# Front buffers in halves of ring slots, low parts written in place, and another form of router and first gather

## What is computed

```python
x1 = x + merged @ w_out
h2 = rms_norm(x1, norm2_g, NORM_EPS).reshape(B * S, D)
logits = (x2 @ w_router + b_router).astype(jnp.float32)      # x2 is h2
top_vals, top_idx = lax.top_k(logits, TOP_K)                  # 4 of 32
top_w = jax.nn.softmax(top_vals, axis=-1)
for e in range(N_EXPERTS):
    a = clamped_swiglu(x2 @ w_up[e] + b_up[e])
    out = out + combine[:, e:e + 1] * (a @ w_down[e] + b_down[e])
return x1 + y
```

## Time and profile before

| | |
|---|---|
| median of 3 runs | 1201.33 us (1199.94 to 1201.79) |
| profiled execution, its own time | 1200.07 us |
| its span, first to last instruction | 1198.3 us |
| PE busy | 1132.7 us (95%) |
| DVE, ACT, POOL busy | 387.5, 279.0, 81.7 us |
| bytes read from HBM | 448.12 MB |
| mean rate, rate from 300 us on | 376, 426 to 427 GB/s |

### The profile page before, as it was taken

How to read it: one execution, slowest core, us unless ns; L and a number is a source line. 1 busy time by engine, 2 the same in 40 slices (tenths; PEclk the granted TensorE clock), 3 DMA queues, 4 the chain that set the end, 5 groups by cost and what they waited for, 6 DMA issues and landing times.

```text
span 1198.3 us, 13630 instructions
## 1 busy us (share of the span) xinstructions
PE 1132.7 (95%) x5603; PEld 534.7 (45%) x5603; DVE 387.5 (32%) x711; ACT 279.0 (23%) x432; POOL 81.7 (7%) x98
## 2 busy tenths in 40 slices
PE   8999999999999999999999998999999899999887
PEld 7789988884333333333333333333333333333332
DVE  5767765653222222222222222222222222222222
ACT  6765454442111111111112111111111111111110
POOL 6424350000000000000000000000000000000000
PEclk9999999999999999999999999999999999999999
DMA  8454569868999999999999999999999999999994
GB/s 318 144 176 143 164 222 349 323 246 368 426 426 427 428 427 427 427 426 426 427 427 428 427 427 427 427 427 426 427 428 427 428 426 427 427 426 426 427 427 190
DMA packets 51466, 449.99 MB, mean 376 GB/s; under 512 B 4610, under 2 KB 4738, under 8 KB 26836
## 3 DMA queue, kind: packets, MB, share of 16 engines
q1 hardware_dynamic: 49936, 447.76, 90.4%
q10 hardware_dynamic: 1476, 1.42, 0.5%
HBM read 448.12 MB, written 1.05 MB: 375 GB/s over the span
## 4 chain that ended last, share of the span: by engine, by line
PE 62%; DMA 21%; SPq 8%; DVE 4%; ACT 1%; issue 1%; another core or an unknown queue 1%; POOL 1%; DVEq 0%; POOLq 0%; ACTq 0%
PE aux L1569 23%; DMA ring<-w_up_dram 20%; PE aux L1637 12%; PE acc L1419 12%; SPq L450 8%; PE aux L1500 3%; PE acc L1412 3%; PE acc L1559 2%; PE aux L1512 1%; DVE w_lo L857 1%; PE aux L1589 1%; PE aux L1619 1%; DVE pick_w L1122 1%; POOL rstd L532 1%
## 5 line engine op out<-in xcount | busy, mean ns | idle before, releaser
L1569 PE MATMUL aux<-ring,xgT 128*64 128x512 f32 x2048 | 462.1, 598 | 46.7 <-DMA ring<-w_up_dram 46.0
L1569 PEld LDWEIGHTS aux<-ring,xgT 128*64 128x64 f32 x2048 | 142.8, 137 | 339.7 <-issue 244.3
L1637 PE MATMUL aux<-ring,aT 128*64 128x512 f32 x1024 | 232.2, 596 | 0.0
L1185 DVE TENSOR_SCALAR glu<-aux 128x512 f32<-128x512 f32 x32 | 22.1, 691 | 396.5 <-PE aux L1569 396.5
L857 DVE TENSOR_TENSOR w_lo<-raw,w_hi 128x1024 fp32r<-128x1024 f32 x80 | 104.3, 1324 | 49.5 <-ACT w_hi L648 49.5
L1637 PEld LDWEIGHTS aux<-ring,aT 128*64 128x64 f32 x1024 | 68.5, 136 | 115.6 <-issue 110.1
L824 ACT ACTIVATE sig<-glu 128x512 f32<-128x512 f32 x32 | 20.2, 630 | 411.8 <-DVE glu L1185 411.8
L648 ACT ACTIVATE w_hi<-raw 128x1024 fp32r<-128x1024 f32 x80 | 84.1, 1059 | 88.3 <-PE acc L1419 72.9
L830 ACT ACTIVATE y_hi<-aux,slot_w 128x512 fp32r<-128x512 f32 x32 | 22.0, 687 | 259.6 <-PE aux L1637 259.6
L1419 PE MATMUL acc<-w_hi,hT_hi 128*128 128x512 f32 x188 | 75.7, 403 | 1.4 <-DVE hT_lo L869 1.3
L1419 PE MATMUL acc<-w_hi,hT_lo 128*128 128x512 f32 x188 | 73.4, 390 | 0.0
(11 more groups left out here) (281 smaller groups left out, 1023.7 us busy)
## 6 DMA issues: line engine op xcount, KB each, us to landing
ring<-w_up_dram SPq DMA_DIRECT2D x128, 2048.0 KB, 48.7
ring<-w_down_dram SPq DMA_DIRECT2D x64, 2048.0 KB, 49.0
raw<-w_in_dram SPq DMA_DIRECT2D x25, 1024.0 KB, 5.3
raw<-w_branch_dram SPq DMA_DIRECT2D x6, 1024.0 KB, 5.1
raw<-w_kv_dram SPq DMA_DIRECT2D x4, 1024.0 KB, 5.1
raw<-w_out_dram SPq DMA_DIRECT2D x4, 1024.0 KB, 5.2
x<-x_dram SPq DMA_DIRECT2D x2, 512.0 KB, 4.2
raw<-w_in_dram SPq DMA_DIRECT2D x2, 512.0 KB, 6.2
```

The costliest lines, as they stand in the source:

```text
L1569: ins = nc.tensor.matmul(bank[64 * half:64 * half + 64, :], xgT[:, k], w_rows[:, c0 + half * W:c0 + (half + 1) * W], start=(k == 0), stop= ...
L1637: ins = nc.tensor.matmul(bank_cy[64 * half:64 * half + 64, :], aT[:, j, 64 * ff_half:64 * ff_half + 64], w_rows[:, half * W:(half + 1) * W ...
```

## The change

Four edits. (1) The front's weight buffers are laid out over slots 6 to 9, each slot holding one piece buffer `raw[i]` in its lower half; `w_lo[i]` has the same address, so the low part overwrites the raw data. The upper halves hold `merged` (slot 6), `hT_lo` (7) and the two `w_hi` (8, 9). The low part of the second half of z goes to `gate`'s memory. A piece's load waits for the use of piece p-4 instead of its split. (2) SyncE's order of ring loads follows: slot 11 behind piece 12, slot 10 behind 36, slots 6 to 9 as pieces 36 to 39 are used. (3) The router multiplies `wr`, scaled by GpSimd, as 32-column weights with the transposed `x1`, four column groups of 32 at a time; two small products with stacked identities (`ident_rep` now 128 rows) add the groups. The first pick comes from PSUM directly, and the first gather is done by pairs of row groups with `x1` as weights, already transposed, two pairs ahead of item 1 and two inside it. The fillers change from 8, 4, 3 to 1, 3, 1, 6, 3. (4) The first slot that is filled again is loaded in two parts, a row each.

```diff
-WARM_UP, KEEP_UP = 14, (8, 4, 3)
+WARM_UP, KEEP_UP = 14, (1, 3, 1, 6, 3)
...
-                    sp.wait_ge(lo_done, 2 * (p - 4) + 2)
-                sp.dma_start(raw[:, p % 4], piece_source(p)).then_inc(raw_loaded[p % 4], 16)
+                    sp.wait_ge(half_used, 2 * (p - 4) + 2)
+                sp.dma_start(raw[p % 4][:], piece_source(p)).then_inc(raw_loaded[p % 4], 16)
...
+                if p == 12:
+                    load_next(11)
                 if p == 27:
                     sp.wait_ge(aux_ready, JOB["mem_y", MEM_H - 1] + 1)
                     block_read(sp, ("cb",))
-                if p in (27, 29, 31, 33):
-                    load_next((p - 27) // 2)
-                if p == 35:
+                if p in (27, 28, 30, 31):
+                    load_next({27: 0, 28: 1, 30: 2, 31: 3}[p])
+                if p == 33:
                     sp.wait_ge(half_used, 2 * LAST_PIECE[("proj", 1, 1)] + 2)
                     load_next(4)
+                if p == 36:
+                    sp.wait_ge(brow_used, len(bias_chunks))
+                    sp.wait_ge(half_used, 2 * (LAST_PIECE[("gate", 0, 1)] - 1) + 1)
+                    load_next(10)
             sp.wait_ge(half_used, 2 * LAST_PIECE[("proj", 0, 1)] + 2)
             load_next(5)
-            for g, last in ((6, NP - 3), (7, NP - 1)):
-                sp.wait_ge(lo_done, 2 * last + 2)
-                load_next(g)
-            sp.wait_ge(half_used, 2 * NP)
-            for g in (8, 9, 10):
-                load_next(g)
-            sp.wait_ge(logits_ready, 1)
-            load_next(11)
-            for g in range(RING, NEXP * CHUNKS):
+            sp.wait_ge(aux_ready, JOB["zT", 3] + 1)
+            for i in range(4):
+                sp.wait_ge(half_used, 2 * (NP - 4 + i) + 2)
+                load_next(6 + i)
+            first_up = w_up[RING // CHUNKS, 0:UP_ROWS * P, :].rearrange("(p j) n -> p j n", p=P)
+            first_rows = ring[:, 0].rearrange("p (j n) -> p j n", j=UP_ROWS)
+            sp.wait_ge(row_used, 1)
+            sp.dma_start(first_rows[:, 0], first_up[:, 0]).then_inc(row_loaded, 16)
+            chunk_used(sp, 0)
+            sp.dma_start(first_rows[:, 1], first_up[:, 1]).then_inc(slot_loaded[0], 16)
+            for g in range(RING + 1, NEXP * CHUNKS):
                 chunk_used(sp, g - RING)
                 load_next(g)
...
             def logit_products(t, h):
-                for k in range(4 * h, 4 * h + 4):
-                    ins = nc.tensor.matmul(acc[2][:, t * NEXP:(t + 1) * NEXP], h2T[:, k, t * P:(t + 1) * P], wr[:, k],
-                                           start=(k == 0 and t == 0), stop=(k == KD - 1), skip_group_check=True)
+                for i in range(KD // 2):
+                    moving = x1T_a[:, i, t * P:(t + 1) * P] if h == 0 else x1T_b[:, t, i]
+                    ins = nc.tensor.matmul(acc[2 + t][32 * i:32 * i + 32, 0:P], wr[:, h * (KD // 2) + i], moving,
+                                           start=(h == 0), stop=(h == 1), skip_group_check=True)
...
+            for t in range(NT):
+                logit_products(t, 0)
+            transpose_x1_second(0)
+            pe.wait_ge(const_built, built("tables"))
+            keep_up(KEEP_UP[0])
+            transpose_x1_second(1)
+            keep_up(KEEP_UP[1])
+            pe.wait_ge(x1T_act, 2)
+            logit_products(0, 1).then_inc(logit_parts, 1)
+            pe.wait_ge(x1T_dve, 2)
+            logit_products(1, 1).then_inc(logit_parts, 1)
+            keep_up(KEEP_UP[2])
+            for t, ready in enumerate((part_act, part_dve)):
+                pe.wait_ge(ready, 1)
+                ins = nc.tensor.matmul(bank_glu[:, t * NEXP:(t + 1) * NEXP], part[:, t], exp_sel[:, 0:NEXP],
+                                       start=True, stop=True, skip_group_check=True)
             ins.then_inc(logits_ready, 1)
...
-            keep_up(1)
-            gather(1)
-            keep_up(2)
+            def gather_pair(pair):
+
+                bank = pair_bank[pair]
+                for i in range(2):
+                    for t in range(NT):
+                        c = pair * UP_ROWS * P
+                        rows = x1[:, t, c:c + UP_ROWS * P].rearrange("s (p j) -> s j p", j=UP_ROWS)[:, i]
+                        ins = nc.tensor.matmul(bank[:, i * SLOTS:(i + 1) * SLOTS], rows, pick[:, t],
+                                               start=(t == 0), stop=(t == NT - 1), skip_group_check=True)
+                ins.then_inc(pair_gathered, 1)
+
+            keep_up(KEEP_UP[4])
+            pe.wait_ge(pick_ready, 1)
+            for pair in range(2):
+                gather_pair(pair)
...
+                    if first_item and k == 0:
+                        ins.then_inc(row_used, 1)
                     if j == UP_ROWS - 1:
                         ins.then_inc(slot_used[slot_of[c]], 1)
+                    if first_item and k in (0, 1):
+                        gather_pair(2 + k)
...
+            def move_pair(pair):
+                dve.wait_ge(pair_gathered, pair + 1)
+                k = slice(2 * pair, 2 * pair + 2)
+                gain = cols[:, C_G2_UP + 2 * pair:C_G2_UP + 2 * pair + 2].unsqueeze(2)
+                nc.vector.tensor_tensor(xgT[:, k], pair_bank[pair][:, 0:2 * SLOTS].rearrange("p (k s) -> p k s", k=2),
+                                        gain.to_broadcast([P, 2, SLOTS]), ALU.mult).then_inc(pair_ready, 1)
```

More of the change, by code:

```diff
@@ L210, in hybrid_block, with halves_of @@
         yT_lo = [sb("y_fox_lo", [P, KB, SEQ], F32R, r), y_conv_lo, sb("y_mem_lo", [P, KB, SEQ], F32R, r)]
-        raw = sb("raw", [P, 4, KB, W], F32, in_slots(6, 8))
-        w_hi = sb("w_hi", [P, 4, 2, W], F32R, in_slots(8, 9))
-        w_lo = sb("w_lo", [P, 4, 2, W], F32R, in_slots(9, 10))
+        def halves_of(slot):
+            first = start_ring + slot * slot_bytes
+            return Region(nc, first, first + slot_bytes // 2), Region(nc, first + slot_bytes // 2, first + slot_bytes)
+        raw, w_lo = [], []
+        second_half = []
+        for i in range(4):
+            lower, upper = halves_of(6 + i)
+            at = lower.at
+            raw.append(sb(f"raw{i}", [P, KB, W], F32, lower))
+            w_lo.append(sb(f"w_lo{i}", [P, KB, W], F32R, Region(nc, at, upper.at)))
+            second_half.append(upper)
+        merged = sb("merged", [P, NT, D], F32, second_half[0])
+        xs = merged
+        hT_lo = sb("hT_lo", [P, KD, SEQ], F32R, second_half[1])
+        w_hi = [sb(f"w_hi{i}", [P, KB, W], F32R, second_half[2 + i]) for i in range(2)]
         r = in_slots(10, 11)
[L215 to L218, removed]
         gate_sel = sb("gate_sel", [96, 3, P], BF16, r)
@@ L570, in _ @@
             chained(nc.gpsimd.memset(ident_rep[:], 0.0))
-            for g in range(3):
+            for g in range(4):
                 rep = ident_rep[32 * g:32 * g + 32]
@@ L804, in _ @@
                                          accum_out=ss[:, STAT[6] + 2 * t + h:STAT[6] + 2 * t + h + 1]).then_inc(x1_squared, 1)
[L805 to L810, removed]
+                if h == 0:
+                    act.wait_ge(x1T_ready, 1)
+                    nc.scalar.activation(x1T_a[:, 0:2], aux[0][:].rearrange("p (k s) -> p k s", k=2), ACT.Copy
+                                         ).then_inc(x1T_act, 1)
+                else:
+                    act.wait_ge(x1T_ready, 3)
+                    nc.scalar.activation(x1T_b[:, 0], aux[2][:].rearrange("p (k s) -> p k s", k=KD // 2), ACT.Copy
+                                         ).then_inc(x1T_act, 1)
+            act.wait_ge(logit_parts, 1)
+            nc.scalar.activation(part[:, 0], acc[2][:, 0:P], ACT.Copy).then_inc(part_act, 1)
             act.wait_ge(top_ready, 1)
@@ L1403, in piece @@
                         k = half * KB + 2 * h + i
+                        lo_k = z_lo[:, k - 4] if kind == "out" and half == 1 else a_lo[:, k]
                         opening = half == 0 and h == 0 and i == 0
                         closing = last and h == 1 and i == 1
-                        wh, wl = w_hi[:, s % 4, i], w_lo[:, s % 4, i]
+                        wh, wl = w_hi[p % 2][:, 2 * h + i], w_lo[p % 4][:, 2 * h + i]
                         if kind in ("cu", "cc", "cb"):
@@ L1461, in _, with keep_up @@
+                return ins
+            def keep_up(times):
+                for _ in range(times):
+                    nc.tensor.matmul(bank_lin[:], ones_bf[0:96], bias_up[:, 0:W], start=True, stop=True)
             pe.wait_ge(x1_squared, 2)
-            pe.wait_ge(h2T_act, 1)
-            pe.wait_ge(h2T_dve, 1)
-            pe.wait_ge(wr_loaded, 16)
-            logit_products(0, 0)
-            transpose_x1(1)
-            logit_products(1, 0)
-            pe.wait_ge(h2T_act, 2)
-            pe.wait_ge(h2T_dve, 2)
@@ L1470, in _ @@
-            for t in range(NT):
-                ins = logit_products(t, 1)
-            ins.then_inc(logits_ready, 1)
-            pe.wait_ge(x1_squared, 4)
```

(13 more changed lines are left out.)

146 lines of the change are left out of this document (91 added, 55 removed).

## The result

| | before | after |
|---|---|---|
| median | 1200.82 us (6 runs, 1199.94 to 1201.79) | 1196.71 us (6 runs, 1196.23 to 1196.98) |
| ratio | | 0.9966, interval 0.9956 to 0.9976 |
| profiled execution: own time, span | 1200.07, 1198.3 us | 1196.88, 1195.1 us |

The changed kernel is 4.1 us faster, 0.34%, where 1.6 us was forecast and the prediction took 0.2% as the least that a measurement can tell from no change. Medians of before beside the later runs were 1200.12, 1200.38 and 1200.37, and the changed kernel measured once more gave 1196.75, so 3.6 us is as good a figure as 4.1. The two profiled executions differ by 3.2 us, and that difference is the one that rows can explain.

A forecast was written before the change was run, and what follows sets the result against it. The prediction took the DMA stream of expert weights, 4.94 us a chunk, as the bound. Its start moving from 291.9 (filling) to 290.3 (fifth refill's release) gave 1.6 us: 1201.33-1.6 = 1199.7 us, range 1197.0 to 1202.7.

The forecast's parts named there:

- R(4): TensorE's release for the ring's fifth refill, the first down chunk: forecast 310.1, less 19.8 for four chunks ahead (set back) 290.3.
- the filling's bound: Ring filling before the change, in terms of an unbroken stream 291.9; filling earlier was worth at most 2.4 us.
- The gather pair: First gather, eight instructions with x1 as strided weights: 1.36 us a pair, plus 0.12 for going to full width and back.
- rival (a): First gather: strided weight loads pass as fast as contiguous ones, gain 3.3 us, 1198.0; chance 0.30.
- The front: Pieces before the router, low parts in place: cost 0, TensorE ending the last piece at 271.87 as before.
- The queue count: Front loads followed behind ring chunks: worst landings 7.6, 8.6 and 9.1 us; ScalarE late once by half a microsecond, TensorE never.
- The router: Between last piece and gather: product calls 0.4 us each, logits at 276.4, 0.6 us earlier, TensorE starting the gather at 279.3.
- the two rows: First refilled slot loaded in two rows: set back 284.7, under 290.3, so worth 0.
- Rival (b): First gather: pairs dear, load and stream in series, logits late too; 2.8 us slower, 1204.1; chance 0.06.
- (c): Front: paired buffers make loads wait and meet ring chunks, some 3 us late, gain -1.4, 1202.7; chance 0.06.
- (d): Tail: same stream, but a slow-clock dip behind the last wait goes, 1.5 us, 1198.2; chance 0.08.
- (e): First refill: its rows start the stream at once, the fifth refill doesn't bind; 7.2 us earlier, 1194.1; chance 0.05.

The follow-up runs named there:

- before_again: The unchanged kernel before, run again for a second trace: 1200.41 us, ratio 1.0002.
- late_fill: The changed kernel with ring chunks 8 to 11 issued as late as before the change: 1201.40 us, ratio to before 1.0009.
- three_late: The changed kernel with ring chunks 9, 10 and 11 issued when the last front piece is used: 1197.83 us, ratio 0.9976.
- combined: The changed kernel with chunks 0 to 4 spread as before, all gather pairs ahead of item 1, refills of slots 4 and 5 in halves: 1195.06 us.
- pairs_ahead: The changed kernel with all four gather pairs ahead of item 1, none inside it: 1196.46 us, ratio 0.9967.
- down_halves: The changed kernel with the fifth refill (slot 4, a w_down chunk) loaded in two halves: 1195.91 us, ratio 0.9965.
- delay_item1: The changed kernel with 12 filler products (2.6 us) in item 1 ahead of its last up chunk: 1199.51 us.
- one_load: The changed kernel with the first refilled slot loaded in one piece when both rows are used: 1197.09 us, ratio 0.9972.
- delay_item2: The changed kernel with 12 filler products in item 2 behind its first step: 1198.02 us.
- ring_spread: The changed kernel with ring chunks 0 to 4 behind pieces 27, 29, 31, 33 and 35 as before the change: 1196.30 us, ratio 0.9965.

## Why the prediction was wrong

The frame held: a stream of 4.94 us a chunk, started by whichever is latest of filling and releases. From R(4) of the changed kernel, 309.31+1.2, 174 chunks of 4.94 and 1.25 to the wait's end give 1171.3; the trace has 1171.40. The forecast of 1.6 us was the difference of two bounds, and **two terms of that sum were mis-sized, to the same side: the filling's bound and the price of the gather pairs in R(4)**. A third part, the landings, stood in no step of the sum. The measured 1196.71 lies 0.3 us under the range's lower end, 1197.0.

- **The filling's bound, 291.9: too early.** The step "continuous transfer begins at about 273.3" took the ramp from one window. The next one moved 328 GB/s, not 427, another 0.5 us: 292.4. The run with the late filling shows such a ramp too. The 2.4 us "at most" was thus 2.9.
- **The bound behind it, R(4) set back 290.3: too late.** It came at 309.31, set back 289.55, 0.75 us earlier. Within it, three terms miss.

  *The gather pair*, forecast at 1.36 us, with 0.12 for going to full width and back: it took 1.02 ahead of item 1 and 1.08 inside. The two ahead took 2.03 us instead of 2.8, and from item 1's first product to R(4) it took 2.5 us more than before instead of 3.0. I took the transposes with the same stride as the nearest row. The pairs' weight loads take 196 ns at stride two:

```profile
L1589 PEld LDWEIGHTS aux<-pick,x x16: 194/196/197, 279.8 to 281.6; 128*128 128x128 f32 x16
```

  The router's contiguous matmul loads in the kernel before:

```profile
L1457 PEld LDWEIGHTS acc<-wr,h2T x32: 187/192/193, 271.6 to 276.6; 128*128 128x128 f32 x32
```

  Here the strided loads cost hardly more; the slow strided loads were those of transposes. The kind of instruction was the better neighbour, and rival (a), with its 1198.0, the better forecast.

  *The front*, forecast at 0 us: the last piece ended 1.1 us late, at 273.0 in place of 271.87, 0.2 to 0.7 us of it by ring chunks ahead of pieces. The queue count had piece 32 landing 9.1 us after its issue; ScalarE waited 5.56 us for it, until 221.1, 12 us after the issue at 209.06. The cover of 5.8 us took most of that, not all.

  *The router*: the calls took 0.29 us each, not 0.4; the gather started 6.8 us after the last piece, not 7.4.

  Front +1.1, router -0.6, pairs -0.8 and -0.5 make the 0.8 us by which R(4) was earlier than forecast, so errors also cancelled.
- **What the sum did not hold.** With both corrected it gives 292.4-289.55 = 2.9 us. The bytes say 2.3 against before's first trace, so 0.6 of the corrected sum is not seen, and 3.0 against its second (86.16 MB), whose own R(4) was late by the slow clock. The spans differ by 3.2 and 3.9. The rest, about 0.9 us in both, was in no step: it is the landings, below.

Right were: R(4) as the release that binds (fillers ahead of it, and halves), the two rows worth nothing, and the DMA running dry after the filling and ahead of R(1) and R(4), with nothing idle after 312 us. Rival (b) fell with the pairs' price, (c) was real but a third of its size, (d) had a price that the traces bear out and the wrong cause for it, and (e) fell as shown.

**What the bytes do not give.** Take the last wait's end (L) and the bytes moved by 330 us (B). The changed kernel's two traces have L = 1171.40 and 1171.16 at B = 87.44 and 87.51. From there 427 GB/s predicts L from B for the others, and the last column of the table says how much later L was.

The traces hold the rest. Each ring load raises its semaphore sixteen times, and the trace keeps the time of each among its semaphore events (no view of the profile prints them; I read them from the trace). There are 16 DMA engines, and I take each event for the share of one of them, though the events don't name it. TensorE's wait ends with the last. For the load that L waits for, the sixteen events of before spread over 8.0 us (1166.58 to 1174.54), those of the changed kernel over 6.7 (1164.70 to 1171.36). The first two columns say how far the last event was behind the mean of the sixteen.

| trace | behind the mean near 358 us | behind the mean at L | L later than B allows |
|---|---|---|---|
| changed kernel, twice | 1.6, 1.3 us | 3.4, 3.3 us | 0 (taken as the base) |
| before | 1.2 | 4.4 | 0.9 |
| before_again | 2.5 | 4.2 | 0.9 |
| late_fill | 1.2 | 4.5 | 1.2 |
| three_late | 3.3 | 5.1 | 1.7 |
| combined | 2.1 | 4.0 | 0.6 |
| pairs_ahead | 1.4 | 3.8 | 0.4 |
| down_halves | 1.2 | 3.7 | 0.2 |
| delay_item1, one_load | 1.1, 1.7 | 3.4, 3.5 | 0.0, 0.0 |
| delay_item2, ring_spread | 1.9, 1.4 | 3.2, 3.2 | -0.2, -0.3 |

The third number is the second less 3.4, to within 0.2 us, in every trace. **So the 0.9 us are not in the stream's mean rate or start: they are one late landing in sixteen.** The shares fall behind in steps. From one load to the next an event comes 4.90 us later, except for steps in which it is 1.4 to 1.6 us more; from 330 us on, the last of the sixteen makes them in before at 488, 706, 938 and 1169.6 us, in the changed kernel at 536, 753 and 990. The step at 1169.6 is the late wait of before, and late_fill has one at 1171.4. The 4.94 us a chunk of the prediction are 4.90 and such steps. Before and late_fill are late by a fourth step shortly ahead of the end; before_again and three_late carry their lag from the start (2.5 and 3.3 us near 358 us).

**What stays open.** Why one share stops for 1.4 us, and why at those times, no run shows. The kernels that lie latest are those whose stream never stood still after the filling, while the changed kernel and those like it stop at 282 us, and it may be that a gap brings the shares level. But before and late_fill were as level near 358 us as the changed kernel, so this can hold for before_again and three_late at most.

At the end about half the engines are busy for some 6 us, in the changed kernel from 1174 on. The share, last but one, falls to about a half and stays there, as the spread of the sixteen events says:

```profile
1172.00:1174.00 2.00, 2.00 (x12) 0.60 (x10) 0.61 (x1) 0.00 (x0) 0.00 (x0) 1.00 0.96 410
1178.00:1180.00 2.00, 1.83 (x14) 1.14 (x14) 1.68 (x6) 1.19 (x2) 0.00 (x0) 1.00 0.46 197
```

## What to carry to other kernels

When a prefetch ring feeds the whole second half of a kernel, write each refill's release minus its place in the stream as one list, together with the time at which the filling is through: the largest entry moves the end, and its distance to the second largest is the most that removing it can bring. Where two entries lie within about 1 us of each other, the runs here gave less than that. Read the ramp of a burst from several windows. Before a wait is taken as ordinary, compare it with its like (2.6 us against 1.25 here), and look how far the last of a load's landings is behind the others. For an unseen instruction take the row of the same kind (a matmul's weight load) before one of the same shape or stride, and where a forecast is a difference of two bounds, carry the error of each into the range.

## What was not expected of the hardware

- Weight loads of float32 matmuls took 196 ns at stride two against 187 to 193 ns contiguous, while those of transposes took 209 ns strided and 140 contiguous. The Trainium skill, "TensorE: Matmul & The Clock Gate", section LDWEIGHTS, counts columns alone, which gives 107 ns for 128. None of these loads took 107 ns; that the layout hardly matters holds in these traces for matmuls and not for transposes.
- Four column groups of 32 passed 16 float32 instructions of 128 columns in 0.58 us, 36 ns each, where full-width ones took 117.
- The sixteen landings of one load spread over 1.6 to 4.4 us near 358 us and over 6.5 to 9 us at the end. The last one fell behind in steps of about 1.4 us, four times in before and three times in the changed kernel from 330 us on, and TensorE waits for it.
